# RWKV-7 triangular inverse: the running transpose made by TensorE in each level, level products spread over four array tiles

## The chip, the cores and the metric

The kernel runs on one core of a Trainium2 chip. The metric is the device time of one execution in microseconds, the median of the runs; lower is better. "A record" below is one matmul instruction of the profile; every fp32 product of 64x64 tiles shows two of them, a transpose of 128x128 one.

## The reference, cut to what matters

The program is a two-layer encoder trunk on 512 positions. The change touches one part of layer 1, RWKV-7 time mixing, whose recurrence is, for 8 heads of width 64:

```python
def step(S, inp):
    r_t, w_t, k_t, v_t, kk_t, a_t = inp
    sa = jnp.einsum("bhvk,bhk->bhv", S, -kk_t)
    S = S * w_t[:, :, None, :] + sa[..., None] * (kk_t * a_t)[:, :, None, :] + v_t[..., None] * k_t[:, :, None, :]
    return S, jnp.einsum("bhvk,bhk->bhv", S, r_t)
```

The kernel computes it in chunks of 64 positions. In a chunk, each `sa` depends on the earlier ones through a strictly triangular 64x64 matrix A per head, so the kernel needs X, the inverse of (I - A), 64 times (8 chunks, 8 heads).

## The kernel before, in words

The 512 positions are four steps t = 0 to 3 of 128 rows. A tile of 128 partitions holds two chunks: c = 0 in partitions 0 to 63, c = 1 in partitions 64 to 127; its 512 columns are 8 heads of 64. `quad(c)` is the slice of 64 partitions (or columns) of number c. X, XT, Y1, ot0, ot1 and A are such 128x512 tiles; all lie in the buffer that the profile calls `slot`.

The inverse is built by doubling: X starts as the inverse of the 2x2 diagonal blocks, and each of five levels n = 0 to 4 doubles the block. A level needs Y1 = (part of A below the present blocks) times X, and then adds X times Y1 to X. TensorE multiplies the transpose of its first operand (`lhsT`), so the second product needs XT, the transpose of X. The kernel before keeps XT as a second running matrix: it is set up by VectorE from A (two operations per t), and each of the levels 0 to 3 computes a product Y1-by-XT and adds it to XT.

So a level of t was:

- TensorE, 16 products `at(ot)` x `at(X)` in two halves of four heads, into `acc[0]` and `acc[1]` (signals `y1_full`);
- ScalarE, line 1868, copies each half to Y1 (`y1_ready`);
- TensorE, 16 products XT x Y1 into a bank, then (not in level 4) 16 products Y1 x XT into another;
- VectorE adds the first bank to X and the second to XT (`dx_used`).

Helpers record the operations, so the profile gives their lines: `mm` is line 694, `tp` (transposes) line 697, VectorE's `tt` line 2035. `each` runs h over heads and c over 0, 1, and both the rows of the array (where the operands lie) and its columns (where the output lies) are `quad(c)`.

The order of the work on each engine is written out by hand. While t is inverted, pieces of t+1 are made: on TensorE `prepare(t+1, n)` stands behind level n = 0, 1, 2 (transposes of r and k; transposes of v and the low-rank products; running sums of the decays and `chunk_sum`), and the transposes `outputs_by_feature(t-1)` behind level 3. ScalarE has the matching copies behind its copies of each level: behind those of level 2 a table load and two sigmoids, behind those of level 3 a table load and four exponentials (line 1811, `exp_ready`), behind those of level 4 the squares for the latent attention (t = 0 and 1). VectorE does, between its level mask and its additions, `masked_scores` (level 0), `gated` (levels 0 and 1, t at least 1), and `prepare(t+1, n-2)` for n = 2 to 4. At t = 3 there is no t+1: TensorE has `latent_rows` (20 transposes) behind level 0 and two `queries` behind each other level.

PSUM banks are handed out by `tile(name, count)`, a ring of four (`turn_banks`): whoever opens a bank waits until the reader of the bank's former content, four openings ago, has signalled. Each `tile` call below is one opening: `rkv_ready`, `wa_sum`, `g_ready`, `exp_ready` (the third of the running sums, read by the fourth exponential), `end_ready`, `ycT_ready`, and the level's own.

Of the kernel before, what the change touches and what calls it, by code (L numbers as in the profile page):

```python
# [13 lines left out]
P = 128  # L14
# [216 lines left out]
def hybrid_trunk(nc, x, positions, e_norm_mix, e_w_in, a_rel_bias, b_conv_w, b_conv_b, b_dt_bias,  # L231
# [5 lines left out]
    with ctx:  # L237
# [6 lines left out]
        def sem(name):  # L244
            name = COUNTS_ON.get(name, (name,))[0]
            if name not in sems:
                sems[name] = ctx.enter_context(nc.semaphore(name))
            return sems[name]
# [109 lines left out]
        F["wt"] = R["wt"].rearrange("p (a b) -> p a b", b=P)  # L358

# [323 lines left out]
        def _(pe):  # L683
# [324 lines left out]
            if upto >= 4:  # L1008
# [115 lines left out]
                for t in range(NT):  # L1124
# [42 lines left out]
                    for n in range(5):  # L1167
                        if n == 0:
                            pe.wait_ge(sem("inv_ready"), t + 1)
                        else:  # L1170

                            pe.wait_ge(sem("dx_used"), 9 * t + 2 * n - 1)
                        for half in range(2):

                            if t or n:
                                pe.wait_ge(sem("y1_ready"), 10 * t + 2 * n + half - 1)
                            each(acc[half], at(f"ot{n % 2}"), at("X"), half).then_inc(sem("y1_full"), 1)
                        if n > 0:
                            pe.wait_ge(sem("dx_used"), 9 * t + 2 * n)
                        b, former = tile("dx_used", 9 * t + 2 * n + 1)  # L1180
                        pe.wait_ge(*former)
                        if n == 0:
                            pe.wait_ge(sem("xt_ready"), t + 1)
                        for half in range(2):
                            pe.wait_ge(sem("y1_ready"), 10 * t + 2 * n + half + 1)
                            m = each(b, at("XT"), at("Y1"), half, half == 0)
                        m.then_inc(sem("dx_full"), 1)
                        if n < 4:
                            b, former = tile("dx_used", 9 * t + 2 * n + 2)
                            pe.wait_ge(*former)  # L1190
                            each(b, at("Y1"), at("XT")).then_inc(sem("dx_full"), 1)
# [14 lines left out]
                    pe.wait_ge(sem("dx_used"), 9 * t + 9)  # L1206
# [281 lines left out]
        def _(act):  # L1488
# [277 lines left out]
            if upto >= 4:  # L1766
# [77 lines left out]

                for piece in range(4):
                    prepare(0, piece)
                for t in range(NT):
# [16 lines left out]
                    for n in range(5):  # L1864
                        for half in range(2):
                            cols = slice(256 * half, 256 * half + 256)
                            act.wait_ge(sem("y1_full"), 10 * t + 2 * n + half + 1)
                            act.activation(R["Y1"][:, cols], acc[half][:, cols], ACT.Copy).then_inc(sem("y1_ready"), 1)
# [162 lines left out]
        def _(dve):  # L2031
# [269 lines left out]
            if upto >= 4:  # L2301
# [143 lines left out]
                for t in range(NT):  # L2445
# [8 lines left out]
                    step(tt(by_head(R["XT"]), by_head(R["A"]), over_heads(level_mask[:, 0, :]), ALU.mult))  # L2454
                    tt(by_head(R["XT"]), by_head(R["XT"]), over_heads(eye64[:, :]), ALU.add).then_inc(sem("xt_ready"), 1)
                    dve.wait_ge(sem("xt_ready"), t + 1)
                    for n in range(5):
# [8 lines left out]
                        dve.wait_ge(sem("dx_full"), 9 * t + 2 * n + 1)  # L2466
                        tt(R["X"], R["X"], bank["dx_used", 9 * t + 2 * n + 1][:, :], ALU.add).then_inc(sem("dx_used"), 1)
                        if n < 4:

                            dve.wait_ge(sem("dx_full"), 9 * t + 2 * n + 2)  # L2470
                            tt(R["XT"], R["XT"], bank["dx_used", 9 * t + 2 * n + 2][:, :], ALU.add).then_inc(sem("dx_used"), 1)
                        dve.wait_ge(sem("dx_used"), 9 * t + (2 * n + 2 if n < 4 else 9))
# [302 lines left out]
```

## Time and profile before

| | |
|---|---|
| runs | 2446.77, 2454.19, 2454.20 us; median 2454.19 |
| profiled execution | span 2445.0 us (its own device time is not given apart; the lowest run is 1.8 us above it) |
| TensorE matmul busy | 2294.9 us, 94% |
| TensorE weight loads | 1950.7 us, 80% |
| VectorE busy | 1169.5 us, 48% |
| ScalarE busy | 943.6 us, 39% |
| mean granted TensorE clock | 0.976 |

The 16 products of level 0 of t = 0 begin at 839.84 us; the last products of this part end near 1030 us, and behind them TensorE goes on without a gap of half a microsecond until 1060 us. A matmul is modelled as busy until its end, so a busy share near 1 of TensorE doesn't say that the array is full. In the views by time a row gives start, duration, engine, line, operation, output and inputs, shapes and count; in square brackets the idle time of the engine before it and what ended that.

### The profile page before, as it was taken

The numbers are of one execution on the slowest core, as the hardware profiler recorded it, in microseconds if no ns is written. First come the engines' busy times: TensorE is split into PE (matmuls) and PEld (weight loads), VectorE is DVE, ScalarE is ACT, GpSimd is POOL, SyncE is SP. The second block draws the span as 40 slices with busy tenths as digits, with TensorE's granted clock in tenths as the row PEclk, the third lists the DMA queues.
The fourth block names the chain that finished last, engine by engine and source line by source line (L and its number), as shares of the span: only waits on it lengthen the run. The fifth ranks groups of instructions, "written<-read, shape, count | busy, mean of one in ns | idle before, by whom it ended". The sixth has DMA issues, their size and how long they took to land.

```text
span 2445.0 us, 37907 instructions
## 1 busy us (share of the span) xinstructions
PE 2294.9 (94%) x15465; PEld 1950.7 (80%) x15465; DVE 1169.5 (48%) x1545; ACT 943.6 (39%) x1176; POOL 118.6 (5%) x179
## 2 busy tenths in 40 slices
PE   7998899999989888888899999999999998999995
PEld 6864888888877777657777777777789998999995
DVE  3266442323244587553478888888885000001001
ACT  4247332222243354253266767676764000000001
POOL 6011000000000000000000000000000000000000
PEclk9989899999999999999899999999999999999998
DMA  6320223242222000110299999999998877877663
GB/s 192 112 83 1 70 90 101 86 142 78 95 86 65 19 3 3 36 35 1 92 370 351 364 355 359 355 361 355 361 360 298 272 260 235 267 243 259 227 225 114
DMA packets 262116, 451.16 MB, mean 185 GB/s; under 512 B 8359, under 2 KB 148494, under 8 KB 261854
## 3 DMA queue, kind: packets, MB, share of 16 engines
q1 hardware_dynamic: 257216, 435.73, 51.4%
q0 software_dynamic: 4576, 13.41, 2.3%
q8 instruction: 107, 1.75, 0.3%
q14 instruction: 27, 0.22, 0.0%
q10 hardware_dynamic: 190, 0.05, 0.0%
HBM read 436.63 MB, written 12.52 MB: 184 GB/s over the span
## 4 chain that ended last, share of the span: by engine, by line
PE 50%; DVE 2%; ACT 2%; issue 1%; DMA 0%; DVEq 0%; POOLq 0%; SPq 0%; ACTq 0%; POOL 0%
PE bank L694 48%; PE bank L697 2%; DVE w_low L2035 1%; ACT w_high L1953 1%; DVE small L2092 0%; DVE arena L2035 0%; DMA xs<-sum_rows_d 0%; DMA sum_rows_d<-arena,idx_now 0%; DVE arena L2753 0%; ACT arena L1590 0%; DVE arena L2099 0%; ACT xg_high L1959 0%; ACT arena L1582 0%; ACT arena L1968 0%; DVE y_low L2035 0%
## 5 line engine op out<-in xcount | busy, mean ns | idle before, releaser
L2035 DVE TENSOR_TENSOR w_low<-slot,w_high 128x2048 fp32r<-128x2048 f32 x172 | 393.6, 2291 | 331.2 <-ACT w_high L1511 265.6
L694 PE MATMUL bank<-arena 128*128 128x144 f32 (+6 forms) x2672 | 356.9, 298 | 9.2 <-ACT arena L1590 4.5
L694 PEld LDWEIGHTS bank<-arena 128*128 128x128 f32 (+4 forms) x2672 | 316.2, 183 | 25.6 <-issue 11.2
L694 PE MATMUL bank<-arena,slot 128*128 128x144 f32 (+4 forms) x2368 | 309.3, 300 | 9.9 <-issue 5.2
L2035 DVE TENSOR_TENSOR arena<-arena,bank 128x512 f32<-128x512 f32 (+2 forms) x99 | 58.7, 593 | 528.2 <-PE bank L694 528.2
L694 PEld LDWEIGHTS bank<-arena,slot 128*128 128x128 f32 (+2 forms) x2368 | 286.1, 182 | 29.1 <-issue 22.3
L2035 DVE TENSOR_TENSOR w_low<-arena,w_high 128x2048 fp32r<-128x2048 f32 x105 | 239.9, 2289 | 25.7 <-ACT w_high L1953 25.0
L694 PE MATMUL bank<-w_high,xg_high 128*128 128x512 f32 x560 | 227.3, 406 | 6.3 <-DVE w_low L2035 4.2
L1953 ACT ACTIVATE w_high<-slot 128x2048 fp32r<-128x2048 f32 x108 | 206.2, 1915 | 69.5 <-PE bank L694 39.3
L694 PE MATMUL bank<-h_ffn,w_high 128*128 128x512 f32 (+1 forms) x736 | 222.6, 385 | 3.1 <-DVE h_ffn L2035 3.1
L1953 ACT ACTIVATE w_high<-arena 128x2048 fp32r<-128x2048 f32 x105 | 201.1, 1920 | 61.7 <-PE bank L694 61.6
L1511 ACT ACTIVATE w_high<-slot 128x2048 fp32r<-128x2048 f32 x64 | 122.2, 1910 | 256.4 <-PE bank L694 256.4
L694 PE MATMUL bank<-w_high,xg_low 128*128 128x512 f32 x560 | 221.1, 395 | 0.0
L694 PE MATMUL bank<-w_low,xg_high 128*128 128x512 f32 x560 | 220.7, 394 | 0.0
L1994 ACT ACTIVATE arena<-bank 128x288 f32<-128x288 f32 (+1 forms) x42 | 17.8, 423 | 484.6 <-PE bank L694 484.6
L694 PE MATMUL bank<-h_mix,w_high 128*128 128x512 f32 (+1 forms) x608 | 178.2, 378 | 11.6 <-DVE h_mix L2035 11.6
L694 PEld LDWEIGHTS bank<-h_ffn,w_high 128*128 128x128 f32 x736 | 135.6, 187 | 34.1 <-issue 2.6
L697 PE MATMUL bank<-ident,arena 128*128 128x128 f32 (+6 forms) x796 | 134.8, 289 | 27.0 <-DVE arena L2099 7.6
L697 PEld LDWEIGHTS bank<-ident,arena 128*128 128x128 f32 (+6 forms) x796 | 99.8, 145 | 64.7 <-issue 11.8
L694 PE MATMUL bank<-h_ffn,w_low 128*128 128x512 f32 (+1 forms) x368 | 141.6, 385 | 0.0
L694 PEld LDWEIGHTS bank<-h_mix,w_high 128*128 128x128 f32 x608 | 112.9, 195 | 34.3 <-issue 8.3
L694 PEld LDWEIGHTS bank<-w_high,xg_high 128*128 128x128 f32 x560 | 105.3, 188 | 32.6 <-DVE w_low L2035 8.6
(368 smaller groups left out, 3321.2 us busy)
## 6 DMA issues: line engine op xcount, KB each, us to landing
slot<-in_moe_w_up_dram SPq DMA_DIRECT2D x86, 1024.0 KB, 6.3
arena<-in_moe_w_gate_dram SPq DMA_DIRECT2D x78, 1024.0 KB, 6.2
arena<-in_moe_w_down_dram SPq DMA_DIRECT2D x64, 1024.0 KB, 5.3
slot<-in_moe_w_down_dram SPq DMA_DIRECT2D x48, 1024.0 KB, 5.4
slot<-in_moe_w_gate_dram SPq DMA_DIRECT2D x34, 1024.0 KB, 5.1
arena<-in_moe_w_up_dram SPq DMA_DIRECT2D x26, 1024.0 KB, 5.6
slot<-in_e_w_in_dram SPq DMA_DIRECT2D x12, 1024.0 KB, 5.8
slot<-in_ff_w_gate_dram SPq DMA_DIRECT2D x11, 1024.0 KB, 5.3
```

The costliest lines, as they stand in the source:

```text
L694: return pe.matmul(o, lhsT, rhs, start=start, stop=True, skip_group_check=True)
L697: return pe.transpose(o, i, ident[0:rows, 0:rows])
L1511: act.activation(w_high[s % DENSE_SPLIT][:, 0:SLOT], slots[n % DENSE_RAW][:, 0:SLOT], ACT.Copy).then_inc(sem("dense_high_ready"), 1)
L1953: act.activation(w_high[n % SPLIT][:, :], raw[:, :], ACT.Copy).then_inc(sem("w_high_ready"), 1)
L1994: act.activation(pair_of(sil_e[:, j % 2, :], cap), pair_of(turn_banks[2 * j % 4][:, 0:2 * CAP], cap), ACT.Silu)\
L2035: return dve.tensor_tensor(o, a, b, op)
```

## The change

XT is no longer carried. In each level TensorE transposes X (four 128x128 transposes into a bank of their own), ScalarE copies the result to XT, and XT's products, additions and set-up go. The first product's loops run over pairs of heads, chunk c and parity of the head, and put the head's parity in the output partitions (`acc[c][quad(par), ...]`); Y1 comes to lie by feature like a transposed tile. The second product then has the parity in the rows of the array and c in its columns, and each parity has a bank of its own, which VectorE adds to every second head of X. A level opens three banks of the ring and not two.

```diff
                         else:
-
-                            pe.wait_ge(sem("dx_used"), 9 * t + 2 * n - 1)
-                        for half in range(2):
-
-                            if t or n:
-                                pe.wait_ge(sem("y1_ready"), 10 * t + 2 * n + half - 1)
-                            each(acc[half], at(f"ot{n % 2}"), at("X"), half).then_inc(sem("y1_full"), 1)
-                        if n > 0:
-                            pe.wait_ge(sem("dx_used"), 9 * t + 2 * n)
-                        b, former = tile("dx_used", 9 * t + 2 * n + 1)
+                            pe.wait_ge(sem("dx_used"), 10 * t + 2 * n)
+                        if t or n:
+                            pe.wait_ge(sem("y1_ready"), 10 * t + 2 * n)
+                        for pair in range(4):
+                            for c in range(2):
+                                for par in range(2):
+                                    h = 2 * pair + par
+                                    m = mm(acc[c][quad(par), CHUNK * pair:CHUNK * (pair + 1)], at(f"ot{n % 2}")(h, c), at("X")(h, c), pair == 0)
+                                if pair == 3:
+                                    m.then_inc(sem("y1_full"), 1)
+                        b, former = tile("xt_ready", 5 * t + n + 1)
                         pe.wait_ge(*former)
-                        if n == 0:
-                            pe.wait_ge(sem("xt_ready"), t + 1)
-                        for half in range(2):
-                            pe.wait_ge(sem("y1_ready"), 10 * t + 2 * n + half + 1)
-                            m = each(b, at("XT"), at("Y1"), half, half == 0)
-                        m.then_inc(sem("dx_full"), 1)
-                        if n < 4:
-                            b, former = tile("dx_used", 9 * t + 2 * n + 2)
+                        for pair in range(4):
+                            m = tp(b[:, P * pair:P * (pair + 1)], R["X"][:, P * pair:P * (pair + 1)])
+                        m.then_inc(sem("xt_full"), 1)
+                        corrections = []
+                        for par in range(2):
+                            b, former = tile("dx_used", 10 * t + 2 * n + par + 1)
                             pe.wait_ge(*former)
-                            each(b, at("Y1"), at("XT")).then_inc(sem("dx_full"), 1)
+                            corrections.append(b)
+                        pe.wait_ge(sem("y1_ready"), 10 * t + 2 * n + 2)
+                        pe.wait_ge(sem("xt_ready"), 5 * t + n + 1)
+                        for pair in range(4):
+                            for par, b in enumerate(corrections):
+                                for c in range(2):
+                                    m = mm(b[quad(c), CHUNK * pair:CHUNK * (pair + 1)], F["XT"][quad(par), pair, quad(c)],
+                                           F["Y1"][quad(par), pair, quad(c)], pair == 0)
+                                if pair == 3:
+                                    m.then_inc(sem("dx_full"), 1)
...
@@ ScalarE
-                        for half in range(2):
-                            cols = slice(256 * half, 256 * half + 256)
-                            act.wait_ge(sem("y1_full"), 10 * t + 2 * n + half + 1)
-                            act.activation(R["Y1"][:, cols], acc[half][:, cols], ACT.Copy).then_inc(sem("y1_ready"), 1)
+                        for c in range(2):
+                            act.wait_ge(sem("y1_full"), 10 * t + 2 * n + c + 1)
+                            act.activation(F["Y1"][:, :, quad(c)], acc[c][:, 0:256].rearrange("p (a b) -> p a b", b=CHUNK), ACT.Copy)\
+                                .then_inc(sem("y1_ready"), 1)
+                        act.wait_ge(sem("xt_full"), 5 * t + n + 1)
+                        act.activation(R["XT"], bank["xt_ready", 5 * t + n + 1][:, :], ACT.Copy).then_inc(sem("xt_ready"), 1)
...
@@ VectorE
-                    step(tt(by_head(R["XT"]), by_head(R["A"]), over_heads(level_mask[:, 0, :]), ALU.mult))
-                    tt(by_head(R["XT"]), by_head(R["XT"]), over_heads(eye64[:, :]), ALU.add).then_inc(sem("xt_ready"), 1)
-                    dve.wait_ge(sem("xt_ready"), t + 1)
...
-                        dve.wait_ge(sem("dx_full"), 9 * t + 2 * n + 1)
-                        tt(R["X"], R["X"], bank["dx_used", 9 * t + 2 * n + 1][:, :], ALU.add).then_inc(sem("dx_used"), 1)
-                        if n < 4:
-
-                            dve.wait_ge(sem("dx_full"), 9 * t + 2 * n + 2)
-                            tt(R["XT"], R["XT"], bank["dx_used", 9 * t + 2 * n + 2][:, :], ALU.add).then_inc(sem("dx_used"), 1)
-                        dve.wait_ge(sem("dx_used"), 9 * t + (2 * n + 2 if n < 4 else 9))
+                        for par in range(2):
+                            dve.wait_ge(sem("dx_full"), 10 * t + 2 * n + par + 1)
+                            x = by_head(R["X"])[:, par::2, :]
+                            tt(x, x, by_head(bank["dx_used", 10 * t + 2 * n + par + 1][:, 0:256]), ALU.add).then_inc(sem("dx_used"), 1)
+                        dve.wait_ge(sem("dx_used"), 10 * t + 2 * n + 2)
```

On TensorE, from the running sums of level 2 to the end of level 4 at t = 1 (the names in square brackets are the signals that a row waits for; before):

```order
3820 L694 MATMUL bank<-arena,cum_rev 128x512 [waits cb_ready]
3821 L694 MATMUL bank<-chunk_sum,arena 128x2 [waits g_ready]
3822 L694 MATMUL bank<-chunk_sum,arena 128x2 x3
3823 L694 MATMUL bank<-slot 64x64 [waits y1_ready,dx_used]
3827 L694 MATMUL bank<-slot 64x64 [waits y1_ready,dx_used]
3831 L694 MATMUL bank<-slot 64x64 [waits dx_used]
3833 L697 MATMUL bank<-ident,slot 128x128 [waits exp_ready,yc_ready]
3835 L694 MATMUL bank<-slot 64x64 [waits y1_ready,dx_used]
```

The same place in the changed kernel:

```order
3701 L696 MATMUL bank<-arena,cum_rev 128x512 [waits g_ready]
3702 L696 MATMUL bank<-chunk_sum,arena 128x2 [waits xt_ready]
3704 L696 MATMUL bank<-slot 64x64 [waits y1_ready,dx_used]
3706 L699 MATMUL bank<-ident,slot 128x128 [waits dx_used]
3708 L696 MATMUL bank<-slot 64x64 [waits y1_ready,xt_ready,exp_ready,dx_used]
3709 L696 MATMUL bank<-slot 64x64 x15
3710 L696 MATMUL bank<-slot 64x64 [waits y1_ready,dx_used]
3712 L699 MATMUL bank<-ident,slot 128x128 [waits end_ready]
```

The wait for `exp_ready` stood at the transposes behind level 3, and now stands at level 3's second product itself.

On ScalarE, the same stretch before:

```order
321 L1868 ACTIVATE slot<-bank 128x256 x2
322 L1811 ACT_TABLE_LOAD
323 L1811 ACTIVATE arena<-bank 128x512 x4
324 L1813 ACTIVATE small<-bank 128x8
325 L1818 ACTIVATE arena<-bank 128x4x128
326 L1868 ACTIVATE slot<-bank 128x256 x2
```

and in the changed kernel:

```order
329 L1878 ACTIVATE slot<-bank 128x4x64 x2
330 L1881 ACTIVATE slot<-bank 128x512
331 L1821 ACT_TABLE_LOAD
332 L1821 ACTIVATE arena<-bank 128x512 x4
333 L1823 ACTIVATE small<-bank 128x8
334 L1828 ACTIVATE arena<-bank 128x4x128
335 L1878 ACTIVATE slot<-bank 128x4x64 x2
336 L1881 ACTIVATE slot<-bank 128x512
```

The copy of XT stands ahead of the table load, and the exponentials stay behind the level's copies.

## Rows read from the trace of the kernel before

**Rows 1.** By time, TensorE, first products of levels 0, 1 and 2 at t = 0.

```profile
839.84 1.15 PE L694 MATMUL bank<-slot 64*64 64x64 f32 x32 [1.09 <-DVE slot L2035]
...
844.25 3.34 PE L694 MATMUL bank<-slot 64*64 64x64 f32 x96
...
850.23 3.34 PE L694 MATMUL bank<-slot 64*64 64x64 f32 x96
```

**Rows 2.** By time, all engines, level 1 of t = 1.

```profile
890.33 3.34 PE L694 MATMUL bank<-slot 64*64 64x64 f32 x96 [0.94 <-DVE slot L2035]
...
891.06 0.85 ACT L1868 ACTIVATE slot<-bank 128x256 f32<-128x256 f32 x2 [0.92 <-PE bank L694]
891.56 1.97 PEld L694 LDWEIGHTS bank<-slot 64*64 64x64 f32 x64 [0.22 <-issue]
...
893.60 0.66 PE L697 MATMUL bank<-ident,arena 128*128 128x128 f32 x4
...
894.43 1.28 DVE L2035 TENSOR_TENSOR slot<-slot,bank 128x512 f32<-128x512 f32 x2
...
895.16 0.29 PEld L694 LDWEIGHTS bank<-lora,arena 64*128 64x128 f32 x2 [0.68 <-DVE slot L2035]
...
897.27 1.01 PEld L694 LDWEIGHTS bank<-slot 64*64 64x64 f32 x32 [0.76 <-issue]
```

**Rows 3.** Stretches of 10 ns; x is the number of records in flight.

```profile
890.90:890.91 0.01, 0.01 (x7) 0.01 (x5) 0.00 (x1) 0.00 (x0) 0.00 (x0) 1.00 0.00 0
916.07:916.08 0.01, 0.01 (x13) 0.01 (x9) 0.01 (x1) 0.01 (x1) 0.00 (x0) 1.00 0.00 0
...
919.40:919.41 0.01, 0.01 (x4) 0.01 (x3) 0.01 (x1) 0.00 (x0) 0.00 (x0) 1.00 0.00 0
```

**Rows 4.** Groups by line and form, 800 to 1060 us: busy us, mean ns, idle before.

```profile
L1868 ACT ACTIVATE slot<-bank 128x256 f32<-128x256 f32 x40 | 15.1, 385 | 25.2 <-PE bank L694 23.5
...
L1856 ACT ACTIVATE slot<-bank 128x512 f32<-128x512 f32 x8 | 4.5, 608 | 0.3 <-PE bank L697 0.3
...
L2035 DVE TENSOR_TENSOR slot<-slot,bank 128x256 f32<-128x256 f32 x8 | 3.4, 420 | 10.9 <-PE bank L694 10.9
```

**Rows 5.** By time, TensorE and ScalarE, levels 3 and 4 of t = 0.

```profile
857.36 4.40 PE L694 MATMUL bank<-slot 64*64 64x64 f32 x128
...
860.25 2.06 ACT L1811 ACTIVATE arena<-bank 128x512 f32<-128x512 f32 x4
...
862.80 1.15 PE L694 MATMUL bank<-slot 64*64 64x64 f32 x32 [1.04 <-ACT slot L1868]
```

**Rows 6.** By time, TensorE from 862.5 us, the product of X and Z1 at t = 0.

```profile
865.88 1.05 PE L694 MATMUL bank<-slot 64*64 64x64 f32 x29 [0.99 <-DVE slot L2035]
```

**Rows 7.** By time, levels 3 and 4 of t = 1; last the product of X and Z1.

```profile
904.40 3.34 PE L694 MATMUL bank<-slot 64*64 64x64 f32 x96
...
909.50 0.63 PE L697 MATMUL bank<-ident,slot 128*128 128x128 f32 x4 [1.76 <-ACT arena L1811]
...
914.66 1.00 PEld L694 LDWEIGHTS bank<-slot 64*64 64x64 f32 x31 [1.41 <-issue]
```

**Rows 8.** By time, VectorE, level 0 of t = 1: the two additions.

```profile
889.59 1.28 DVE L2035 TENSOR_TENSOR slot<-slot,bank 128x512 f32<-128x512 f32 x2
```

**Rows 9.** By time, TensorE, the running sums behind level 2 of t = 1.

```profile
900.85 1.12 PE L694 MATMUL bank<-arena,cum_excl 128*128 128x512 f32 x2 [0.24 <-ACT arena L1805]
```

**Rows 10.** By time, TensorE at t = 3: latent rows, level 4's second product.

```profile
989.56 4.53 PE L697 MATMUL bank<-ident,arena 128*128 128x128 f32 x20 [3.31 <-DVE arena L2352]
...
1019.59 1.15 PE L694 MATMUL bank<-slot 64*64 64x64 f32 x32 [1.58 <-ACT slot L1868]
```

**Rows 11.** Stretches: length, busy us of PE, PEld, DVE, ACT, POOL, clock, DMA.

```profile
827.80:831.20 3.40, 0.03 (x1) 0.00 (x0) 3.19 (x7) 1.84 (x5) 0.00 (x0) 1.00 0.00 0
831.20:834.60 3.40, 3.00 (x14) 3.00 (x15) 3.35 (x6) 1.33 (x3) 0.00 (x0) 0.50 0.00 0
...
933.73:937.00 3.27, 3.27 (x62) 3.27 (x64) 3.17 (x6) 0.77 (x2) 0.00 (x0) 0.50 0.00 0
```

More of the change, by code:

```diff
@@ L358, in hybrid_trunk @@
         F["wt"] = R["wt"].rearrange("p (a b) -> p a b", b=P)
+        F["XT"] = R["XT"].rearrange("p (a b) -> p a b", b=P)
+        F["Y1"] = R["Y1"].rearrange("p (a b) -> p a b", b=P)
         bonus = [small[:, 192:200], small[:, 240:248]]
@@ L1205, in _ @@
                     each(b, lambda h, c: F["ak"][quad(c), h, 0:CHUNK], at(f"v{t % 2}")).then_inc(sem("zu_full"), 1)
-                    pe.wait_ge(sem("dx_used"), 9 * t + 9)
+                    pe.wait_ge(sem("dx_used"), 10 * t + 10)
                     pe.wait_ge(sem("z_ready"), 4 * t + 1)
@@ L1843, in rstd_of @@
                     act.activation(small[:, 216:224], small[:, 216:224], ACT.Sqrt).then_inc(sem("gn_rstd"), 1)
+                quad = lambda c: slice(CHUNK * c, CHUNK * (c + 1))
                 for piece in range(4):
```

## The prediction

> **What bounds the kernel now.** I read the page first (TensorE 94% busy, VectorE 48%), then the view by time over the inverse, 840 to 1030 us. A busy share says little there: records overlap. What counts is the order of first products. At t = 0 they start at 839.84, 844.25, 850.23 and 857.36 us [rows 1, 5]; between them TensorE does the level and then its filler for t+1, mostly without idling. In rows 2 the reader sees a level: both halves of the first product from 890.33, ScalarE's copies of them at 891.06 (0.73 us after the start) to 891.91, the other two products from 891.56, the filler from 893.60. So a level occupies TensorE for 3.27 us, and the next first product can come as soon as VectorE has added to X. TensorE's in-order stream is the limit in most levels, with three exceptions: VectorE at level 0 for t of at least 1, where the additions come at 889.59 and TensorE waits 0.94 us [rows 2, 8], and again inside the filler of level 1, where a bank is freed late (0.68 us idle before the second low-rank product, 0.76 before level 2 [rows 2]); ScalarE behind level 2, whose sigmoids TensorE waits for [rows 9]; and ScalarE in levels 3 to 4, where a table load and four exponentials (2.06 us) delay level 4's copies at t = 0 and the transposes of rows 7 at t = 1 (1.76 us idle). Behind 1030 us TensorE never idles for half a microsecond before the attention starts, so I carry a shift of the inverse to the end at 1:1.
>
> **Part 1, the products.** In flight at one instant, with records of 218 ns, are 7 in a level's product, which uses two tiles of the array (both chunks on the diagonal), 13 where two products with the columns alternating overlap, and 4 where a product stays in one tile [rows 3]. That is one record per 31, 17 and 54 ns: four tiles run at once. The new loops visit all four tiles in turn, so 32 records cost 0.5 us in place of 0.96 to 1.0 (bounds for one product: 0.47, half of the present one, and 0.96, no gain). I take 0.5, which is nearest to the 17 ns.
>
> **Part 2, the chain of a new level**, from its first record. Both chunks' signals now come with the last pair of heads. Rows 2 give 0.27 us from a half's last record to its copy, so the copies run from 0.75; two back to back of 0.385 us [rows 4] with 0.26 between starts end at 1.4. The four transposes start at 0.6 and take 0.59 (893.60 to 894.19 for four such, of which rows 2 show 0.66 with the tail), so they hide under these copies. Then XT's copy, 0.61 us for a 128x512 copy [rows 4], ends at 1.9. TensorE restarts about 0.1 later, at 2.0, and is free at 2.5: **0.75 us less than the 3.27 of a level now**, although 0.9 us of it are idle. VectorE adds twice 0.42 us [rows 4] from 2.7, so the next first product can start at 3.6; where no filler stands between, that is a loss against the 3.27 now.
>
> **Part 3, VectorE.** Off go two set-up operations per t and four additions of 128x512 (1.28 us for two [rows 8]); five further ones become ten of 0.42. At level 0 for t of at least 1, where VectorE is the limit, that is 1.4 us of set-up before the additions (two operations of 0.69).
>
> **Part 4, the bank ring.** A level opens three banks of four. Openings of level 2's filler and level 3 are now: exponential's bank, `end`, XT, parity 0, parity 1. The fifth falls on the first one's bank. The second product of level 3 therefore waits for `exp_ready`, as the order of the instructions shows, and that signal is ScalarE's fourth exponential, which stands behind level 3's own copies. At t = 0 to 2 the chain of level 3 becomes: copies to 1.9, table load 1.3 (857.36 + 0.73 + 0.85 to 860.25 [rows 5]), exponentials 2.06, so 5.2; the second product 5.3 to 5.8; additions to 6.9; level 4's first product at 6.9; its second 8.9 to 9.4. Queued behind the waiting product are `outputs_by_feature`, level 4 and everything after it; VectorE's `prepare(t+1, 2)` starts at 6.9 and ends near 10.1, so the last additions end at 10.9. At t = 0 and 1 ScalarE's squares and Z1's copy follow the copies of level 4; at t = 0 that takes from about 862.9 to 865.88, 3.0 us [rows 5, 6], and now it follows XT's copy, which ends at 8.8. The product of X and Z1 starts at 11.8 us from the start of level 3. It stands at 8.5 for t = 0 (865.88 less 857.36 [rows 5, 6]) and 10.3 for t = 1 [rows 7]. **Loss: 3.3 and 1.5 us, and I take t = 2 like t = 1.**
>
> **The sum**, per t, in us (minus is faster):
> - t = 0: level 0 now takes 4.4; new 3.6: -0.8. Level 1 now 6.0; new 2.6 and the same filler, 5.3: -0.7. Level 2: the table load before the sigmoids starts at 1.9 and not 1.58: +0.3. Levels 3 and 4: +3.3. Together +2.1.
> - t = 1: level 1 starts when X is complete; VectorE gets there 1.4 us of set-up earlier, and two additions of 0.42 stand in the place of X's one of 0.69: -1.2, of which I keep -1.1. Level 1: the second low-rank product still waits for VectorE (895.16, 4.8 us after the level's start [rows 2]); VectorE comes 0.6 earlier since XT's addition ahead of `gated` is gone, and 0.3 since its addition is short: -0.9. Level 2 +0.3, then +1.5. Together -0.2. The same for t = 2.
> - t = 3: the latent rows wait for VectorE now (3.31 us idle [rows 10]); 1.4 us of set-up and 0.4 of additions less: -1.8. Levels 1 to 3, each followed by long queries: -0.9, -0.7, -0.7. Level 4's copies wait for ScalarE (1.58 idle [rows 10]), and XT's copy is now behind them: +0.3. Together -3.8.
>
> That is -2.1 us. The clock takes some of it back. Before 831.20 TensorE had done nothing for 3.4 us, and the next 3.4 us ran at 0.50, that is 1.2 GHz [rows 11]; the 2.06 us of exponentials and the load leave TensorE idle for 4 us in level 3, three times. Level 0 of t = 2 ran mostly at 0.50: 62 records in flight in 3.27 us [rows 11], where 96 take 3.34 [rows 2]; the missing 34 come at 31 ns each, 1 us late. Three times 1 us (bounds 0 and 2 us each) makes +3. Sum: 2445.0 + 0.9, near 2446 in span. The runs' median is 9.2 us above the profiled span for reasons that the trace doesn't show, so I put the difference on the median: **2455 us**. What a measurement of this kernel can tell from no change is about 0.3%, 7.4 us; the runs themselves lie that far apart.
>
> The Trainium skill says in "TensorE: Matmul & The Clock Gate", Part 4, that a transpose doesn't count as work that raises TensorE's clock. The trace disagrees: the 0.50 stretch of rows 11 from 831.20 held transposes alone, and the clock was at 1.00 again from 834.60. By that page the new levels, with 20 blocks of transposes, would run at the lower clock more often; that is the second rival. The same page (Part 1, on the floor between starts) gives about 25 ns between starts of small matmuls; the 17 ns of rows 3 are below it. By that floor each product would take 0.8 us.
>
> **Rivals.**
> 1. *The four tiles don't run at once in a long product* (slower). Each product then takes 0.95 us. On the path lie twice 0.45 in most levels of t = 0 and 3, less where VectorE or ScalarE limits: about +3.4, +2, +2, +3, so +10 on the sum: 2466 us. For: the 13 in flight come from two neighbouring products of 16 records each. Against: nothing in the rows sets two such products apart from one that takes the tiles in turn.
> 2. *The clock stays low in the levels* (slower). TensorE works 1.6 us of each 2.5 in a level. If half of the 130 us of levels ran at 0.50, with about 0.3 us lost per us (1 us in the 3.3 of level 0 at t = 2 [rows 11]), it costs 20 us: 2474. It decides from some 25 us at 0.50 on. Against: dense filler stands between most levels.
> 3. *The exponentials' wait costs little* (faster). If ScalarE's exponentials didn't hold the second product, level 4's second would come at 7.2 and not 9.4, three times 2.2 us less, and no clock loss: -8.7, so 2445.
> 4. *The change moves nothing*, since VectorE and ScalarE already set the pace: inside the forecast's own range.
>
> **How the numbers follow.** Forecast and rival 4 together 0.58 (2448 to 2461), rival 1 0.13, rival 2 0.12, rival 3 0.17. The range reaches down to rival 3 and up past rival 1: 2443 to 2469. Faster by over 0.3%: rival 3 and a little, 0.18. Slower by over 0.3%: rivals 1 and 2 and a little of the forecast, 0.28. The rest, 0.54, is no change.
>
> **What would show it.** Level products of 32 records in 0.7 us with their tail, not 1.15; a level's second product 2.0 us after its first; at level 3 of t = 0 to 2 TensorE idle for some 4 us with ScalarE's exponential line as releaser; the latent rows of t = 3 with their idle time unchanged but 1.8 us earlier. The forecast is wrong if level 3's second product starts at 2.0, if the products take 1 us, or if the clock column of the inverse falls below 0.9 at t = 0 and 1.

## The result and the profile after

| | before | after |
|---|---|---|
| median | 2454.19 us (4 runs, 2446.77 to 2454.24) | 2471.51 us (4 runs, 2468.7 to 2473.2) |
| profiled span | 2445.0 us | 2470.0 us |
| mean granted TensorE clock | 0.976 | 0.966 |

The changed kernel takes 1.0082 of the time before (95% interval 1.0066 to 1.0098): 0.8% slower, 2.5 us above the range of the forecast.

The page's first section, of the changed kernel:

```profile
PE 2298.8 (93%) x15033; PEld 1948.8 (79%) x15033; DVE 1155.3 (47%) x1541; ACT 954.1 (39%) x1196; POOL 116.8 (5%) x179
```

TensorE had 15465 records before and is now busy for as long (2294.9 us before) with 432 fewer, so some of them take longer or overlap less. Where it did shows in the order of time. First a level as planned, level 1 of t = 1 (start, duration, engine, line, operation; its counterpart is [rows 2]):

```profile
908.75 0.69 PE L696 MATMUL bank<-slot 64*64 64x64 f32 x32 [0.26 <-DVE slot L2048]
909.37 0.66 PE L699 MATMUL bank<-ident,slot 128*128 128x128 f32 x4
...
909.48 0.66 ACT L1878 ACTIVATE slot<-bank 128x256 f32<-128x256 f32 x2 [0.24 <-PE bank L696]
910.07 0.60 ACT L1881 ACTIVATE slot<-bank 128x512 f32<-128x512 f32 x1
...
910.81 0.69 PE L696 MATMUL bank<-slot 64*64 64x64 f32 x32 [0.78 <-ACT slot L1881]
...
914.82 0.69 PE L696 MATMUL bank<-slot 64*64 64x64 f32 x32
```

A product takes 0.69 us with its tail, the second starts 2.06 us after the first, and level 2 begins 6.07 us after level 1. It was 6.94 [rows 2].

Then levels 3 and 4 of t = 0, TensorE and ScalarE, the counterpart of [rows 5, 6]:

```profile
862.29 0.69 PE L696 MATMUL bank<-slot 64*64 64x64 f32 x32
...
863.61 0.60 ACT L1881 ACTIVATE slot<-bank 128x512 f32<-128x512 f32 x1
864.22 1.28 ACT L1821 ACT_TABLE_LOAD   x1
865.52 2.06 ACT L1821 ACTIVATE arena<-bank 128x512 f32<-128x512 f32 x4
...
867.68 1.13 PE L696 MATMUL bank<-slot 64*64 64x64 f32 x32 [4.11 <-ACT arena L1821]
869.71 1.13 PE L696 MATMUL bank<-slot 64*64 64x64 f32 x32 [0.90 <-DVE slot L2048]
...
872.67 1.13 PE L696 MATMUL bank<-slot 64*64 64x64 f32 x32 [0.78 <-ACT slot L1881]
...
876.30 1.83 PE L696 MATMUL bank<-slot 64*64 64x64 f32 x29 [0.79 <-issue]
```

The wait for the exponentials is there, 4.11 us, and the second product starts 5.39 us after the first, against a forecast of 5.3. But the same 32 records that took 0.69 us now take 1.13, and those of the product of X and Z1 1.83 where they took 1.05. The stretches say why (length, busy us of PE, PEld, DVE, ACT, POOL, then the granted clock):

```profile
862.50:866.58 4.08, 1.07 (x36) 0.76 (x28) 0.43 (x1) 3.53 (x7) 0.00 (x0) 1.00 0.01 2
866.58:900.71 34.13, 30.07 (x420) 28.63 (x424) 15.02 (x31) 10.64 (x28) 0.00 (x0) 0.50 0.01 1
...
924.60:931.40 6.80, 3.72 (x71) 3.18 (x72) 2.36 (x6) 4.09 (x9) 0.00 (x0) 0.50 0.01 2
```

TensorE did nothing from 863.57 to 867.65. At 866.58, within that time, the clock fell to 0.50, 1.2 GHz, and stayed there for 34.13 us, through level 4, the state products of t = 0 and the start of t = 1. The same wait at t = 1 was followed by 6.8 us.

For a measure that leaves out what happens elsewhere in the program I take **the stage**: from the first product of level 0 at t = 0 to the product of X and Z1 at t = 3. It went from 186.78 us (839.84 to 1026.62) to 204.01 (844.31 to 1048.32), with its clock:

```profile
844.31:1048.32 204.01, 158.68 (x2769) 126.51 (x2769) 124.97 (x261) 90.98 (x191) 0.00 (x0) 0.85 0.03 8
```

```profile
839.84:1026.62 186.78, 161.72 (x3200) 135.82 (x3201) 138.68 (x264) 81.00 (x171) 0.00 (x0) 0.96 0.03 9
```

The second row is of before. The stage lost 17.23 us and the medians differ by 17.32. The profiled spans differ by 25.0, because the profiled execution of before is its fastest (2446.77 us), 7.4 us below its median; the other 7.8 us lie outside the stage (the changed execution already entered it 4.47 us late, and lost about 3 more behind it), where the code is the same. That the stage and the medians agree so closely is therefore in part chance.

### The profile page after: what moved, and what is told of

It is laid out like the page before. It is cut to its first block, busy times and chain, and to the rows that moved or that the text cites. A ratio compares the mean times of both kernels' runs of the same rounds, so it can differ in the third digit from the quotient of the medians.

```text
span 2470.0 us, 37079 instructions
## 1 busy us (share of the span) xinstructions
PE 2298.8 (93%) x15033; PEld 1948.8 (79%) x15033; DVE 1155.3 (47%) x1541; ACT 954.1 (39%) x1196; POOL 116.8 (5%) x179
## 4 chain that ended last, share of the span: by engine, by line
PE 50%; DVE 2%; ACT 2%; issue 1%; DMA 0%; DVEq 0%; POOLq 0%; SPq 0%; ACTq 0%; POOL 0%
PE bank L696 48%; PE bank L699 2%; DVE w_low L2048 1%; ACT w_high L1966 1%; DVE small L2105 0%; DVE arena L2048 0%; DMA xs<-sum_rows_d 0%; DMA sum_rows_d<-arena,idx_now 0%; DVE arena L2761 0%; ACT arena L1600 0%; DVE arena L2112 0%; ACT xg_high L1972 0%; ACT arena L1592 0%; ACT arena L1981 0%; DVE y_low L2048 0%
## 5 line engine op out<-in xcount | busy, mean ns | idle before, releaser
L699 PEld LDWEIGHTS bank<-ident,arena 128*128 128x128 f32 (+6 forms) x796 | 103.5, 150 | 65.2 <-issue 11.8
```

Of the source, the lines that this page charges most:

```text
L699: return pe.transpose(o, i, ident[0:rows, 0:rows])
```

## The experiments

All ten, with the stage beside the median; "before" is the kernel before on the same chip. The stage is read from one profiled execution each. The medians of before differ by up to 2.1 us between the chips, so a difference between two kernels of different rows is uncertain by as much.

| kernel | median us | before | ratio (95%) | stage us | clock in it |
|---|---|---|---|---|---|
| after | 2471.51 | 2454.19 | 1.0082 (1.0066 to 1.0098) | 204.01 | 0.85 |
| `k1_no_ring` | 2457.59 | 2452.23 | 1.0028 (1.0018 to 1.0037) | 185.16 | 0.92 |
| `k2_filled_wait` | 2454.53 | 2452.23 | 1.0010 (0.9999 to 1.0021) | 190.44 | 0.95 |
| `k3_wait_alone` | 2466.04 | 2452.23 | 1.0060 (1.0044 to 1.0077) | 198.90 | 0.93 |
| `k4_two_tiles` | 2497.97 | 2452.23 | 1.0191 (1.0174 to 1.0208) | 227.88 | 0.75 |
| `k5_busy_elsewhere` | 2483.79 | 2454.32 | 1.0129 (1.0104 to 1.0154) | 217.71 | 0.84 |
| `k6_ring_and_fill` | 2451.70 | 2454.32 | 0.9997 (0.9987 to 1.0008) | 183.40 | 1.00 |
| `k7_before_filled` | 2456.35 | 2454.32 | 1.0012 (1.0000 to 1.0024) | 187.72 | 0.98 |
| `k8_one_product` | 2473.16 | 2454.32 | 1.0086 (1.0064 to 1.0107) | 203.95 | 0.86 |
| `k9_fill_sized` | 2439.69 | 2452.18 | 0.9953 (0.9940 to 0.9967) | 176.31 | 0.99 |
| `k10_level3_on_vector` | 2441.73 | 2452.18 | 0.9965 (0.9951 to 0.9979) | 175.27 | 0.99 |

The theory from these rows: the wait is as forecast, and what was sized wrongly is the clock that falls in it. Rivals: the wait itself costs that much, or the new levels have too little work everywhere.

### Is it the wait or the clock: fill the wait

```diff
+                        if t + 1 < NT and n == 3:
+                            pe.wait_ge(sem("y1_ready"), 10 * t + 2 * n + 2)
+                            for i in range(4):
+                                mm(acc[1][:, :], ident[:, :], R["X"], True)
                         corrections = []
```

> The changed kernel with four unused 128x512 products (into acc[1], overwritten later) on TensorE inside the wait of level 3 at t = 0 to 2; the wait itself stays. Theory A, with the clock as the larger part: the clock stays at 1.00 behind the wait, the state products of t = 0 run at full rate, and 10 to 14 us come back though nothing waits for less: 2457 to 2462 us. Rival (the waiting itself costs the time): no gain, 2468 to 2474 us.

Level 3 of t = 0 with the unused products, and the stretch behind it:

```profile
862.01 3.70 PE L696 MATMUL bank<-slot,ident 128*128 128x512 f32 x8 [0.15 <-ACT slot L1882]
...
865.96 0.69 PE L696 MATMUL bank<-slot 64*64 64x64 f32 x32 [0.26 <-issue]
```

```profile
865.90:900.00 34.10, 26.62 (x652) 23.55 (x652) 26.57 (x51) 14.56 (x37) 0.00 (x0) 1.00 0.01 2
```

The second product still starts 5.39 us after the first (860.57 to 865.96), so the wait is untouched. The clock stays at 1.00, 2.4 GHz, and the 34 us hold 652 records in place of 420. The stage is 13.6 us shorter than the changed kernel's and the median 17.0 us lower (15.0 us, when each is taken against its own before). With TensorE working in the wait, to no use, the kernel is at before's time; with the wait empty it is 15 to 17 us slower. So by far the greater part of the loss is the clock.

### The wait without the new levels

The kernel before, with the wait put ahead of its second product at level 3:

```diff
+                        if t + 1 < NT and n == 3:
+                            pe.wait_ge(sem("exp_ready"), 4 * (t + 1) + 4)
```

> The kernel before, with one wait added: at level 3 of t = 0 to 2 the second product waits for the fourth exponential, as in the changed kernel. XT is carried as before. Theory A: TensorE idles for some 3.7 us there; the wait costs 2 to 4 us at t = 0 and about 2 at t = 1 and 2, and if the clock falls afterwards as in the changed kernel another 5 to 12: 2460 to 2474 us. Rival (the wait needs the rest of the change to cost anything): under 3 us, below 2457.

TensorE idles 4.06 us, and the clock falls here too, for 6.8 us:

```profile
862.87 6.02 PE L694 MATMUL bank<-slot 64*64 64x64 f32 x128 [4.06 <-ACT arena L1813]
```

```profile
859.95:866.78 6.83, 3.91 (x74) 3.94 (x75) 0.88 (x2) 2.73 (x6) 0.00 (x0) 0.50 0.01 2
965.77:972.60 6.83, 5.36 (x82) 4.94 (x83) 2.16 (x8) 1.88 (x5) 0.00 (x0) 0.50 0.00 0
```

The stage grows by 12.1 us: 5.0, 3.5 and 4.5 us in the parts of t = 0, 1 and 2, less 0.9 us at t = 3, where it has fewer low stretches than before's. The wait is enough to make the kernel slower without any of the new levels, but no stretch of 34 us comes with it.

### The changed kernel without the wait

The corrections go into the unused halves of `acc`, so a level opens one bank of the ring:

```diff
-                            b, former = tile("dx_used", 10 * t + 2 * n + par + 1)
-                            pe.wait_ge(*former)
+                            b = bank["dx_used", 10 * t + 2 * n + par + 1] = acc[par][:, 256:512]
```

> The changed kernel, but the corrections go to the upper halves of acc[0] and acc[1] and open no bank of the ring; everything else is the same. Theory A (the wait for the exponentials' bank leaves TensorE idle for 4.1 us at level 3, and the low clock that follows costs the rest): level 3's second product starts 2.0 us after its first at t = 0 to 2, level 4's first 3.6 us after, level 4's copies still wait for ScalarE until about 5.4; no idle time over 3 us in TensorE at t = 0, the clock stays at 1.00 through t = 0, and the kernel gains 10 to 18 us on the changed one: 2453 to 2461 us. Rival (the low clock comes from the sparser levels as such, not from the one wait): the clock still falls at t = 0 or 1, and the time stays above 2465 us.

Level 3 and the second product of level 4, t = 0:

```profile
860.24 0.69 PE L696 MATMUL bank<-slot 64*64 64x64 f32 x32
...
862.30 0.69 PE L696 MATMUL bank<-slot 64*64 64x64 f32 x32 [0.78 <-ACT slot L1880]
...
866.79 0.69 PE L696 MATMUL bank<-slot 64*64 64x64 f32 x32 [1.61 <-ACT slot L1880]
```

The second product is free at 2.06 us. The exponentials now delay level 4's copies, 1.6 us. The stage is 1.6 us shorter than before's, though its clock is lower (0.92 against 0.96). The median is yet 5.4 us above before's: its profile shows, at the start of the attention, whose code is the same, a 0.50 stretch that of the other profiles only `k3_wait_alone` has (there at 1078.41):

```profile
1066.61:1073.44 6.83, 6.51 (x20) 4.29 (x20) 3.65 (x11) 4.69 (x13) 0.00 (x0) 0.50 0.00 0
```

Whether that stretch is chance or a consequence, these runs do not settle. A further 6 us of this execution lie in one wait near its end, also in unchanged code: TensorE idles 11.16 us before 2053.58, and 5.1 to 5.3 us at the same place in the other profiles.

### Two tiles at a time

The loops of both products reordered, so that only two tiles of the array alternate:

```diff
-                        for pair in range(4):
-                            for c in range(2):
+                        for c in range(2):
+                            for pair in range(4):
...
-                        for pair in range(4):
-                            for par, b in enumerate(corrections):
+                        for par, b in enumerate(corrections):
+                            for pair in range(4):
```

> The changed kernel with the loops of both level products reordered, so that two tiles of the array (one row group, both column groups) work at a time and not four; same products, banks and signals. If four tiles at once are worth what the trace of the changed kernel shows (0.47 us less for each product), each product takes 0.94 us again, but the first chunk's and first parity's signals come early, so the chain of a level grows by only 0.3 to 0.7 us: 5 to 12 us slower than the changed kernel, 2476 to 2484. Rival (the array's rate is hidden behind ScalarE's copies): within 3 us of the changed kernel. More TensorE activity might also keep the clock up, which would show as a faster time and a higher clock.

```profile
868.35 0.98 PE L696 MATMUL bank<-slot 64*64 64x64 f32 x32
...
874.02 1.61 PE L696 MATMUL bank<-slot 64*64 64x64 f32 x32 [4.11 <-ACT arena L1821]
```

```profile
870.65:908.15 37.50, 31.55 (x420) 30.11 (x424) 15.19 (x31) 13.04 (x30) 0.00 (x0) 0.50 0.01 2
```

A product takes 0.98 us at the full clock, against 0.69 with four tiles; the loss is 26.5 us on the changed kernel, two to five times what was expected. Of it 23.9 us are in the stage. Twenty levels with two products, each 0.3 us longer at the full clock, would be 12 us; the other 12 us go with the lower clock, 0.75 against 0.85, which is an estimate: no run takes the two apart. Working on two tiles kept TensorE busy longer (185.9 us of the stage against 158.7) and the clock lower.

### Work elsewhere, and less work in the wait

If the levels only lacked work, it could stand anywhere. Behind the filler of level 1, the wait left empty:

```diff
+                        if t + 1 < NT and n == 1:
+                            for i in range(16):
+                                mm(acc[1][:, 0:P], ident[:, :], cum_incl[:, :], True)
```

> The changed kernel, wait of 4.08 us at level 3 left empty, with 16 unused products of 128x128 by 128x128 put behind the filler of level 1 (t = 0 to 2), where TensorE is busy anyway. They cost about 1.9 us on the path each time, 5 to 6 us. Theory (an empty wait lowers the clock, and only work inside the wait keeps it): nothing is won, the changed kernel's 2471.5 plus 5, so 2474 to 2480, and a stretch of over 20 us at 0.50 behind at least one of the waits. Rival (what the changed kernel lacks is work on the array in general, wherever it stands): the clock stays up as with the filled wait, 2454.5 plus 5, so 2457 to 2463. If the wait is filled by chance no better and the long stretch at half clock of the first trace was an accident of one execution, the median would stay near 2471 plus 5 all the same; the trace then shows no stretch over 10 us.

```profile
869.94:904.07 34.13, 28.18 (x402) 27.07 (x403) 13.74 (x28) 10.89 (x28) 0.00 (x0) 0.50 0.01 1
```

Nothing is won: 12.3 us slower than the changed kernel, and the long stretch is back. (The 16 products take 3.7 us here and not the 1.9 expected, 0.23 us each; three times that is 11.)

One product of 128x512 in the wait in place of four:

> The changed kernel with one unused product of 128x512 in the wait of level 3 and not four: it fills 0.4 to 0.9 us of the 4.08 and leaves more than 3 us empty. Theory (the length of the idle stretch decides): most of the loss stays, 2465 to 2473, with half-clock stretches of some 7 us or more behind the waits. Rival (a little work in the wait is enough): 2453 to 2458, as with four.

```profile
863.53 1.12 PE L696 MATMUL bank<-slot,ident 128*128 128x512 f32 x2 [0.16 <-ACT slot L1881]
867.48 1.13 PE L696 MATMUL bank<-slot 64*64 64x64 f32 x32 [2.83 <-issue]
```

```profile
866.36:900.49 34.13, 30.05 (x420) 28.61 (x424) 15.03 (x31) 10.63 (x28) 0.00 (x0) 0.50 0.01 1
```

2.83 us of idle time remain, and the whole loss with them: median and stage are those of the changed kernel. Together the two rule out that a little more work is enough, or work at any place. Of the fillings tested, only the one that left 0.4 us of the wait empty kept the clock up behind it; how much less would do was not tested.

### Filling what is left

On `k1_no_ring`, unused 128x128 products behind the transposes of level 0 to 2 (and of 3 at t = 3), of level 4, and ahead of the latent rows. They go into `acc[2]`, which nobody reads there:

```diff
+                        if n == 4 and t + 1 < NT:
+                            pe.wait_ge(sem("exp_ready"), 4 * (t + 1) + 1)
+                        if n != 3 or t + 1 == NT:
+                            for i in range(12 if n == 4 else 6):
+                                mm(acc[2][:, 0:P], ident[:, :], cum_incl[:, :], True)
                         corrections = []
...
                             if n == 0:
+                                for i in range(16):
+                                    mm(acc[2][:, 0:P], ident[:, :], cum_incl[:, :], True)
                                 latent_rows()
```

> The kernel without the ring banks (2457.6, its inverse stage about 1 us shorter than before's) with unused 128x128 products in the waits that are left: 6 behind the transposes of levels 0 to 2 (and 3 at t = 3), 12 at level 4, 16 ahead of the latent rows. They take the time in which TensorE waits (0.8, 1.6 and 2.5 us). Theory (what is left of the loss is the clock): the short stretches at 0.50 in levels go, 3 to 8 us less, 2449 to 2455, at or below before's 2452. Rival (the rest is the chain of the new level, and the unused products delay what is behind them): 2458 to 2464. A drop in the attention stage, as at 1066.6 us in the last trace, would stay in either case.

```profile
841.27:1024.67 183.40, 164.33 (x3052) 137.73 (x3053) 124.38 (x260) 88.47 (x191) 0.00 (x0) 1.00 0.03 9
```

The clock is at 1.00 through the stage, and the median 2.6 us below before's, not told apart from it. But the products were longer than the waits:

```profile
863.59 2.84 PE L696 MATMUL bank<-cum_incl,ident 128*128 128x128 f32 x24
...
866.37 0.69 PE L696 MATMUL bank<-slot 64*64 64x64 f32 x32
```

Level 4's second product starts 3.89 us after its first (862.48) and waits for nothing but them; it was 2.90 without (863.89 to 866.79). So the counts were cut, 6 to 3, 12 to 6 (9 at t = 3), 16 to 9:

> The filled kernel without ring banks, with the unused products cut to what the waits hold. A 128x128 one takes 0.23 us (24 records in 2.76 us in its trace), so 12 of them at level 4 were 1 us longer than the wait, and 6 in the other levels 0.5 us longer. Now 3 in levels 0 to 2, 6 at level 4 (9 at t = 3), 9 ahead of the latent rows. Theory (their surplus was on the path): 3 times 1 us, 11 levels of up to 0.5 us and 1.2 us at the latent rows come off, 6 us below 2451.7 at the most: 2444 to 2450, and so below before's 2454 by 0.2 to 0.4%. Rival (the surplus was what kept the clock up, and with exact filling the 0.50 stretches come back): 2452 to 2457.

```profile
861.73 1.50 PE L696 MATMUL bank<-cum_incl,ident 128*128 128x128 f32 x12
...
863.51 0.69 PE L696 MATMUL bank<-slot 64*64 64x64 f32 x32 [0.28 <-ACT slot L1887]
```

```profile
840.39:1016.70 176.31, 151.95 (x2919) 124.47 (x2919) 124.02 (x260) 88.57 (x191) 0.00 (x0) 0.99 0.03 9
```

2439.69 us: 12.5 us below before, 0.9953 (0.9940 to 0.9967). The version **beats both kernels**. The clock is nearly as good as with twice the products (0.99 against 1.00), and 7.1 us of surplus are gone from the stage; the parts of t = 0 to 3 are 0.1, 3.0, 1.9 and 5.5 us shorter than before's.

As a control, the kernel before with 8 such products in its 1.76 us wait of [rows 7]:

```diff
                         if t >= 1 and n == 3:
+                            for i in range(8):
+                                mm(acc[0][:, 256:256 + P], ident[:, :], cum_incl[:, :], True)
                             outputs_by_feature(t - 1)
```

> The kernel before with 8 unused products of 128x128 ahead of the transposes behind level 3 at t = 1 to 3, where TensorE waits 1.7 us for ScalarE's exponentials at t = 1 and 2. Theory (only long waits cost clock; before's waits of 1 to 1.7 us leave 0.50 stretches of 3.4 us alone): no difference, 2450 to 2455; at t = 3 they cost up to 1 us. Rival (filling gains wherever something is filled, so that the gain of the filled kernel says nothing on the change): 2440 to 2448.

It is the same or 0.1% slower, so filling this wait does not win by itself. The control leaves before's other waits empty, above all the 3.31 us ahead of the latent rows [rows 10]. Behind it before's clock is at 0.50 for 6.8 us (988.1 to 995.1), and the 20 transposes there take 4.46 us up to the next product, against 2.33 in `k9_fill_sized`; with 0.4 us in level 1 that is 2.6 us. So at most 2.6 of the 10.5 us by which the sized kernel's stage is shorter could also be had without the new levels. The rest is put down to them, once their waits cost no clock; a kernel before with every wait filled was not run.

Last, XT's copy of level 3 moved to VectorE:

```diff
+                        if n == 3:
+                            dve.wait_ge(sem("xt_full"), 5 * t + n + 1)
+                            dve.tensor_copy(R["XT"], bank["xt_ready", 5 * t + n + 1][:, :]).then_inc(sem("xt_ready"), 1)
```

> The same, with XT's copy of level 3 made by VectorE, which is idle there, so that ScalarE's table load and exponentials begin 0.6 us earlier and level 4's copies, which follow them, too. Theory (ScalarE's queue sets the start of level 4's copies at t = 0 to 2): 3 times 0.6 us off the sized kernel, 1 to 2 us, 2443 to 2449. Rival (VectorE is late at level 3 of t = 1 and 2, since its prepare pieces stand ahead of the copy, and level 3's second product waits): 1 to 3 us more than the sized kernel.

```profile
857.91 1.28 ACT L1827 ACT_TABLE_LOAD   x1
858.70 0.59 PEld L696 LDWEIGHTS bank<-slot 64*64 64x64 f32 x32 [1.15 <-ACT slot L1884]
858.74 0.69 PE L696 MATMUL bank<-slot 64*64 64x64 f32 x32 [0.94 <-DVE slot L2485]
```

The load starts 1.40 us after the level's first product (856.51) and not 1.94 (858.90 less 856.96 in the sized kernel), but the second product 0.17 us later, 2.23. The stage is 1.0 us shorter, the median 2.0 us higher (2438.8 to 2447.0 against 2438.7 to 2444.3), so a gain is not shown.

## Why the prediction failed

By its own steps, in the stage's parts. A part runs from one product of X and Z1 to the next; the first begins with level 0.

| part | before | after | change | forecast without clock | change with the wait filled |
|---|---|---|---|---|---|
| t = 0 | 26.04 | 31.99 | +5.95 | +2.1 | +3.83 |
| t = 1 | 48.82 | 59.16 | +10.34 | -0.2 | +1.45 |
| t = 2 | 48.25 | 50.80 | +2.55 | -0.2 | +0.06 |
| t = 3 | 63.67 | 62.06 | -1.61 | -3.8 | -1.68 |
| sum | 186.78 | 204.01 | +17.23 | -2.1 | +3.66 |

- **Part 1, the products: right.** 32 records take 0.69 us with a tail of 0.22, so 0.47 from start to start, at the lower bound. Rival 1 falls: at two tiles the product takes 0.98, and that is what `k4_two_tiles` shows and the changed kernel does not.
- **Part 2, the level's chain: right.** The second product at 2.06 (forecast 2.0), XT's copy 0.60 (0.61), level 2 after 6.07 us (-0.87; forecast -0.9). The latent rows of t = 3 come 5.60 us after level 0's start and not 7.58, 2.0 earlier (forecast 1.8), with 2.85 us of idle time; it had been put down as unchanged at 3.31 [rows 10].
- **Part 4, the ring: right**, wait, releaser and places. With the wait filled, X times Z1 starts at t = 0 11.86 us after level 3's start (860.57 to 872.43); the forecast was 11.8. Removing the wait takes 5.3 us off the stage (190.44 to 185.16, with the clock at 0.95 and 0.92); the forecast had 3.3 + 1.5 + 1.5.
- **The sum without clock: within 0.6 us, once the clock is taken off.** The last column says +3.66 where -2.1 was forecast, but the filled kernel still has five low stretches in its stage, 20.5 us, and before has three, 13.7 us. What they cost can be read beside the same piece of work at 1.00. In the filled kernel: 1.4 us at t = 0 (levels 0 and 1 take 10.54 us, and 9.09 in `k1_no_ring`), 1.7 at t = 1 (level 2 with its filler 9.17 us, and 7.47 at t = 0), 0.3 at t = 2 (levels 0 and 1 10.40 us, and 10.10 at t = 1), and 4.3 at t = 3 (the latent rows 4.46 us, and 2.33 in `k9_fill_sized`; level 1 7.28, and 6.75 in `k1_no_ring`; the last queries 5.68, and 4.07 in `k9_fill_sized`). In before: 2.6 us, all at t = 3. Without these costs the four parts change by about +2.4, -0.3, -0.2 and -3.4, together -1.5 us. What is left of a miss is at t = 3: in the changed kernel levels 1 to 3 brought 0.43, 0.59 and 0.58 us and not 0.9, 0.7 and 0.7, and level 4's second product came at 3.49 us where it was 2.73 (+0.76, forecast +0.3).
- **The step that failed is the clock's term**, "Three times 1 us (bounds 0 and 2 us each) makes +3". The clock behind the waits alone cost 13.6 (204.01 less 190.44), and with the low stretches that remain in the filled kernel about 18.7 (17.23 and 1.5). Two things in it were wrong. It supposed that each wait would be followed by one stretch of some 3.3 us; the first was followed by 34.13 us. And its price of 1 us came from level 0 of t = 2 [rows 11], where the slower products cost nothing: level 1 begins 5.43 us after level 0 there and 5.42 at t = 1, at the full clock. In both it begins 0.7 us after VectorE starts its additions (938.41 to 939.16, 889.59 to 890.33), so VectorE sets its start. The trace of before had dearer stretches to go by, which the prediction did not use. Behind its longest wait in the stage, 3.31 us ahead of the latent rows, 6.8 us at 0.50 cost 2.6 us, more than the upper bound of 2. And outside the stage, from 1189.5 us, it has one low stretch of 20.5 us that begins while TensorE works on products of 8 columns (`w_router`).
- **Rival 2** had the right cause, and the right price by luck, since the row it took it from cost nothing: it put 0.3 us of loss on each us at 0.50, and 13.6 us went with some 41 us more at 0.50 than in the filled kernel (61.4 against 20.5 in the stage), but put it in the levels at large and against it the dense filler between them. The stretch ran through the state products, behind level 4, where no filler of this kind stands. Its sign, a clock column below 0.9 in the inverse at t = 0 and 1, is what came. The range ended at 2469 and so left out this rival's own 2474, although it had a chance of 0.12.
- **Rival 3** (without the wait 8.7 us less) gave the faster side its chance. Removing the wait brings 13.9 us on the medians of the changed kernel, and with the other waits filled 31.8. Against before, where the rival had 8.7 us, the stage without the wait is 1.6 us shorter, and 10.5 with the other waits filled.
- **Rival 4**, no change, falls: the interval of the ratio, 1.0066 to 1.0098, leaves out 1.

The two low stretches of before that are named above, and the latent rows' transposes at the full clock in `k9_fill_sized` (before's are in [rows 10]):

```profile
988.20:994.90 6.70, 5.34 (x36) 5.01 (x38) 5.41 (x26) 3.44 (x5) 0.00 (x0) 0.50 0.00 1
...
1189.60:1210.00 20.40, 16.49 (x60) 13.54 (x60) 9.49 (x34) 0.23 (x1) 0.00 (x0) 0.50 0.34 135
```

```profile
983.16 2.41 PE L699 MATMUL bank<-ident,arena 128*128 128x128 f32 x20 [0.63 <-DVE arena L2371]
985.49 0.69 PE L696 MATMUL bank<-slot 64*64 64x64 f32 x32
```

The Trainium skill, "TensorE: Matmul & The Clock Gate", section "Why this matters for your kernels", warns of idle gaps between bursts of matmuls because the engine drops to its lower clock. The runs agree, and add what the gap is worth here: 15 to 17 us for three gaps of 4.1 us each.

## What to carry to other kernels

A wait on TensorE has two prices: its length, if it is on the path, and the clock behind it. Here the second was more than twice the first (13.6 us of the stage against 5.3), and it is not read from a row in which the slower products were hidden behind another engine; so when a change makes a new wait of several microseconds, bound the clock's term by the whole of the sparse work that follows, not by one low stretch. Before judging such a change, put unused products into the wait, counted so that they end before it does: that separates the two prices in one run, and here turned a loss of 0.8% into a gain of 0.5% once the wait for a shared bank was also gone.

## What the runs showed of the hardware that I had not expected

- One idle stretch of 4.08 us was followed by 34.13 us at 1.2 GHz, although TensorE was busy for 30.07 us of them; the same stretch at t = 1 and 2 by 6.8 and 3.4 us, and in the kernel before (4.06 us of idle time) by 3.4 to 6.8. With 2.83 us of idle time it was again 34.13. The long one came only at t = 0, in four kernels with the new levels (after, one product, work elsewhere, two tiles: 37.50); two tiles has one more of 17.1 us, from 993.5. What sets t = 0 apart stays open.
- A low stretch cost nothing where another engine set the time anyway (level 0 of t = 2 in before, 5.43 us against 5.42), and about half of its length where products are dense: level 2 of t = 1 in the filled kernel took 1.7 us more with 3.4 us at 0.50 in it.
- Half the array makes things worse twice: a product with two tiles takes 0.98 us and not 0.69, and the stage's clock goes from 0.85 to 0.75.
- Products that nobody uses, on the busiest engine, made the kernel faster. Where they ended before the wait did they cost nothing that these runs tell; where they were longer, their surplus was on the path (7.1 us of the stage between the two filled kernels).
